# Start-up casting loads that wait for the first plain load, and row terms read from one copy in DRAM

## The reference

```python
proj = x @ w_in                                              # (b, l, D_PROJ)
q, k, v, f_logit, z_att, z_ssd, xbc, dt_raw = jnp.split(proj, _split_points(PROJ_SIZES), axis=-1)
log_f = jax.nn.log_sigmoid(f_logit + b_forget)
F = jnp.cumsum(log_f, axis=1)                                # (b, l, 8 heads)
s = einsum(q, k) * scale + (F[t] - F[s])                     # causal, softmax over s, times v
att = att * silu(z_att)
...
dt = softplus(dt_raw + dt_bias)
a_cs = cumsum(dt * A, axis=2)                                # inside chunks of 128 positions, 32 heads
decay = exp(where(causal, a_cs[l] - a_cs[s], -inf))
y = (C.B * decay) @ (x * dt) + state terms + d_skip * x      # then silu(z_ssd) gate and group RMSNorm
...
h = concatenate([att, y]) @ w_out
x = layer_norm(alpha * x + h, ln_g, ln_b)
```

## Time and profile before

| | us |
|---|---|
| median of 3 runs (lowest 1677.67) | 1677.75 |
| own time of the profiled execution | 1675.15 |
| its span on the slowest core, first to last instruction | 1673.6 |
| spans of the eight cores | 1664.3 to 1673.6 |
| PE busy on the slowest core | 1635.6 (98%) |
| DVE, POOL, ACT busy | 1135.5, 883.6, 849.6 |
| share of the DMA engines, q1 and q0 | 31.4% and 23.5% |

### The profile page before, as it was taken

How to read it: one execution, slowest core, us unless ns; L and a number is a source line. 1 busy time by engine, 2 the same in 40 slices (tenths; PEclk the granted TensorE clock), 3 DMA queues, 4 the chain that set the end, 5 groups by cost and what they waited for, 6 DMA issues and landing times.

```text
span 1673.6 us, 31910 instructions; the slowest of 8 cores (1664.3 to 1673.6 us)
## 1 busy us (share of the span) xinstructions
PE 1635.6 (98%) x9108; PEld 801.4 (48%) x9108; DVE 1135.5 (68%) x2342; ACT 849.6 (51%) x1979; POOL 883.6 (53%) x1377
## 2 busy tenths in 40 slices
PE   5999999999999999999999999999999999999997
PEld 2454544544555455445554455455545544444443
DVE  2676777767876887678668876777778666444444
ACT  2767665665665666666666666666566610000000
POOL 2164564655664667468556765656567523222221
PEclk9999999999999999999999999999999999999999
DMA  9955954593457345644652473239556776445431
GB/s 169 149 79 92 134 97 93 114 123 91 104 103 131 81 92 110 112 97 85 126 87 73 89 139 64 54 77 157 110 112 126 197 194 189 138 139 139 139 95 76
DMA packets 180538, 191.33 MB, mean 114 GB/s; under 512 B 118828, under 2 KB 137132, under 8 KB 175980
## 3 DMA queue, kind: packets, MB, share of 16 engines
q1 hardware_dynamic: 164348, 126.89, 31.4%
q0 software_dynamic: 16016, 62.40, 23.5%
HBM read 198.74 MB, written 39.85 MB: 143 GB/s over the span
## 4 chain that ended last, share of the span: by engine, by line
PE 92%; DMA 4%; issue 1%; DVE 1%; ACT 1%; SPq 0%; POOL 0%; another core or an unknown queue 0%; DVEq 0%; ACTq 0%; POOLq 0%
PE bank L544 91%; DMA mixd<-att 1%; DMA xq<-xT 1%; DMA rowb<-arowd 1%; DMA mixd<-yn 1%; DMA xtok<-xsf 0%; SPq L603 0%; DVE xt L577 0%; PE bank L833 0%; ACT L555 0%; SPq L605 0%; PE bank L762 0%; ACT u L555 0%; ACT dec L555 0%; DVE acc L577 0%
## 5 line engine op out<-in xcount | busy, mean ns | idle before, releaser
L544 PE MATMUL bank<-xq,slab 128*128 128x512 bf16 x3072 | 726.0, 380 | 0.0
L544 PE MATMUL bank<-slab,xq 128*128 128x512 bf16 x2048 | 480.7, 379 | 1.1 <-DMA slab<-wpack 1.1
L544 PEld LDWEIGHTS bank<-xq,slab 128*128 128x128 bf16 x3072 | 293.9, 98 | 304.9 <-issue 3.9
L577 DVE SCALAR_TENSOR_TENSOR acc<-u,cst,acc 128x512 f32<-128x512 f32 x384 | 328.1, 857 | 51.5 <-ACT acc L555 38.8
L544 PEld LDWEIGHTS bank<-slab,xq 128*128 128x128 bf16 x2048 | 197.2, 98 | 211.4 <-issue 1.5
L555 ACT ACTIVATE dec<-rowb,nb 128x128 bf16<-128x128 f32 x512 | 202.2, 397 | 28.1 <-PE bank L544 16.2
L555 ACT ACTIVATE P<-bank,boff 128x512 bf16<-128x512 f32 x192 | 131.1, 683 | 68.7 <-PE bank L544 67.8
L544 PE MATMUL bank<-wo,mTa 128*128 128x512 bf16 x704 | 163.7, 379 | 0.0
L555 ACT ACT_TABLE_LOAD x14 | 18.0, 1283 | 273.6 <-DVE st L1169 270.3
L577 DVE SCALAR_TENSOR_TENSOR xt<-xt,bank 128x512 f32<-128x512 f32 x64 | 43.9, 685 | 141.1 <-PE bank L544 140.8
L566 POOL TENSOR_TENSOR xdd<-xtok,dtde 128x256 bf16<-128x256 bf16 x120 | 83.1, 692 | 85.3 <-PE bank L544 62.9
(11 more groups left out here) (113 smaller groups left out, 2197.8 us busy)
## 6 DMA issues: line engine op xcount, KB each, us to landing
slab<-wpack POOLq DMA_DIRECT2D x80, 512.0 KB, 8.7
rowb<-arowd SPq DMA_DIRECT2D x128, 256.0 KB, 4.0
xt<-x_tok SPq DMA_DIRECT2D x16, 1024.0 KB, 5.0
out<-xt SPq DMA_DIRECT2D x15, 1024.0 KB, 4.3
gbc<-growd SPq DMA_DIRECT2D x32, 256.0 KB, 5.2
mixd<-yn SPq DMA_DIRECT2D x128, 64.0 KB, 2.3
xq<-xT POOLq DMA_DIRECT2D x15, 512.0 KB, 33.8
wo<-w_out POOLq DMA_DIRECT2D x11, 512.0 KB, 9.6
```

Of the source, the lines that this page charges most:

```text
L544: fns.append(lambda e, o=o, a=a, b=b, s=s, t=t: e.matmul(o, a, b, start=s, stop=t))
L577: return p.op("dve", [lambda e: e.scalar_tensor_tensor(out=o, in0=a, scalar=s, in1=b, op0=op0, op1=op1)], dve_us(n, nptr) + (0.12 if nptr ...
```

## The change

Every one of the 21 start-up loads gets `behind=sfb`, which becomes `after=`: it must wait for the last writer of `sfb`, the load of `sf`, and for the readers recorded by then, the two casts of `sf` into `fdtw`. Later calls of `slab_load` and `x_load` have no `behind` and stay as they are. `growd` and `arowd` lose the dimension of copies, `copy_rows` and `copies` go, and every read of a row takes the one row for all 128 partitions, behind its store alone.

```diff
-    growd = nc.dram_tensor("growd", [16, 8, L], F32, kind="Internal").ap()
-    arowd = nc.dram_tensor("arowd", [16, 16, 32, 128], F32, kind="Internal").ap()
+    growd = nc.dram_tensor("growd", [8, L], F32, kind="Internal").ap()
+    arowd = nc.dram_tensor("arowd", [16, 32, 128], F32, kind="Internal").ap()
...
-    def slab_load(name, prio, gate=()):
+    def slab_load(name, prio, gate=(), behind=()):
...
-            1 << 20, 300.0 if prio < -990 or name[1] > 1 else 230.0, after=pro_bufs if s >= NSLOT else ())
+            1 << 20, 300.0 if prio < -990 or name[1] > 1 else 230.0, after=pro_bufs if s >= NSLOT else behind)
...
-    def x_load(q, j, prio, gate=()):
+    def x_load(q, j, prio, gate=(), behind=()):
...
-            "xq%d_%d" % (q, j), list(gate), [b_xq[q][j]], prio, 1 << 20, 300.0 if q < 2 else 230.0)
+            "xq%d_%d" % (q, j), list(gate), [b_xq[q][j]], prio, 1 << 20, 300.0 if q < 2 else 230.0,
+            after=behind)
...
-            x_load(it[0], it[1], n - 1000)
+            x_load(it[0], it[1], n - 1000, (), sfb)
         else:
-            slab_load((it, 0), n - 1000)
+            slab_load((it, 0), n - 1000, (), sfb)
...
-    def copy_rows(q, t, gate):
-
-        qs = slice(q * 512, (q + 1) * 512)
-        a = arowd[:, 4 * q:4 * q + 4, :, :].rearrange("k c (g h) l -> (c g) k (h l)", h=4)
-        DMA("sp", [(growd[1:16, :, qs], growd[0:1, :, qs].to_broadcast([15, 8, 512])),
-                   (a[:, 1:16, :], a[:, 0:1, :].to_broadcast([32, 15, 512]))],
-            "rows%d" % q, [b_row1[q], gate], [b_row[q]], t, 1228800, 100.0)
...
-        DMA("sp", [(gb[:, :], growd[ks, i, g * 512:(g + 1) * 512].unsqueeze(1).to_broadcast(shape))], "gbc%d" % r, [brow],
+        DMA("sp", [(gb[:, :], growd[i:i + 1, g * 512:(g + 1) * 512].to_broadcast([128, 512]))], "gbc%d" % r, [b_row1[g]],
...
-            DMA("sp", [(rb[:, :], arowd[ks, c, h4, :].rearrange("k h l -> k (h l)").unsqueeze(1).to_broadcast(
-                shape))], "rowb%d" % k3, [brow], [brb], t - 14, 262144, 200.0)
+            DMA("sp", [(rb[:, :], arowd[c:c + 1, h4, :].rearrange("k h l -> k (h l)").to_broadcast(
+                [128, 512]))], "rowb%d" % k3, [b_row1[q]], [brb], t - 14, 262144, 200.0)
...
-        if i == 1:
-            copy_rows(q, T[0] + 40, b_mix_att[1][q])
```

More of the change, by code:

```diff
@@ L677, in build_program @@
     b_mix_y = [[Buf("my%d_%d" % (g, c)) for c in range(16)] for g in range(8)]
-    b_row = [Buf("rows%d" % q) for q in range(4)]
     b_row1 = [Buf("row%d" % q) for q in range(4)]
-    def copy_rows(q, t, gate):
-        qs = slice(q * 512, (q + 1) * 512)
-        a = arowd[:, 4 * q:4 * q + 4, :, :].rearrange("k c (g h) l -> (c g) k (h l)", h=4)
-        DMA("sp", [(growd[1:16, :, qs], growd[0:1, :, qs].to_broadcast([15, 8, 512])),
-                   (a[:, 1:16, :], a[:, 0:1, :].to_broadcast([32, 15, 512]))],
-            "rows%d" % q, [b_row1[q], gate], [b_row[q]], t, 1228800, 100.0)
-    def copies(i, q):
-        return (slice(0, 1), [1, 128, 512], b_row1[q]) if i < 2 else (slice(0, 16), [16, 8, 512], b_row[q])
     def xpiece(q, j):
@@ L743, in prologue_quarter @@
         qs = slice(q * 512, (q + 1) * 512)
-        DMA("sp", [(growd[0, :, qs], cs[0:8, :]),
-                   (arowd[0, 4 * q:4 * q + 4, :, :].rearrange("c p l -> p c l"),
+        DMA("sp", [(growd[:, qs], cs[0:8, :]),
+                   (arowd[4 * q:4 * q + 4, :, :].rearrange("c p l -> p c l"),
                     cs[32:64, :].rearrange("p (c l) -> p c l", c=4))], "row%d" % q, [bc], [b_row1[q]], pr, 81920, 30.0)
@@ L895, in attention @@
         gb, bgb = GBC[r]
-        ks, shape, brow = copies(i, g)
-        DMA("sp", [(gb[:, :], growd[ks, i, g * 512:(g + 1) * 512].unsqueeze(1).to_broadcast(shape))], "gbc%d" % r, [brow],
+        DMA("sp", [(gb[:, :], growd[i:i + 1, g * 512:(g + 1) * 512].to_broadcast([128, 512]))], "gbc%d" % r, [b_row1[g]],
             [bgb], base - 20, 262144, 200.0)
@@ L971, in ssd @@
         nw, bnw = NW[0]
-        ks, shape, brow = copies(i, q)
         car, bcar = CAR[0]
```

## The result

The changed kernel takes 1703.8 us (median of 4 runs, 1702.37 to 1705.63) beside 1678.7 us of the kernel before in the same job: a ratio of 1.0153, 95% interval 1.0137 to 1.0169, or 25.7 us more (0.0153 x 1678.7). That is inside 2%, but the time lies above the predicted range (1671.7 to 1682.0).

What follows compares the result with a forecast made beforehand. TensorE bounds the kernel, busy 1635.63 of core 1's 1673.60 us, behind the start-up load queue. Hold -0.5, copies -0.1, row reads 0 and order 0 sum to -0.6 us: 1677.1 us from 1677.75, range 1671.7 to 1682.0.

Steps and rivals of the forecast that it cites:

- The hold: Start: GpSimd's first casting load waits until about 8.0, q0's first packet comes at 10.0; the queue ends 0.5 us earlier.
- lower bound of 9.3: Start: earliest first q0 packet after the held issue, 1.3 us later as for a lone load, leaving no gap.
- rival 2: Start: first casting packet takes 5.25 us again, the queue comes 2.8 us later, 1680.4 us; chance 0.16.
- the 1.1 us: Start: gain of the casting queue because its 255 packets from 6 to 16 are cheaper when unmixed with plain ones.
- the forecast's 0.5 us earlier: Start-up queue: gain of 1.1 us from unmixed packets less a gap of 0.6 us before the first casting packet.
- rival 3: Start: order only, packets no cheaper unmixed, so the gap makes it 0.6 us later, 1678.2 us in all; chance 0.12.
- The copies: Four times two transfers within DRAM go; slowest core gains 0.1 us, its distance to core 5, bound 1.5.
- the stall of SP: SyncE stands 16.0 us, up to 376.38, until the store of `att` lands; removing this gains the slowest core 0.1 us.
- The reads of one row: Head groups 2 to 7: 120 loads cost 0.4 us more each, covered by buffers filled ahead; cost 0, uncovered 48 us.
- Rival 4: Head groups 2 to 7: one DRAM row is too slow under load, losing 4.9 us, 1682.0 us in all; chance 0.10.
- The order: All engines to the end: new start times move neighbours; value 0, bounds -4.9 and +4.9 from small stalls of 100 to 430.
- 910 of 910: From 430 to 1340: TensorE busy 910 of 910 us before, and expected to stay so as a sign of being right.

Runs made afterwards that it cites:

- the run without the gate: Kernel before in its exact order, no hold; only the four copies' wait for the store of the attention output is dropped: ratio 0.9996.
- 16 parts: Kernel before in its exact order with its copying; groups 2 to 7 read copy 0 only, in the shape 16 by 8 by 512: ratio 1.0101.
- the other order: Kernel before with no change of work; the scheduler's assumed rate for start-up input loads is 290 for 300, giving a new order: ratio 1.0108.
- Three new orders: Kernel before, order made anew with the hold alone (1.0086), an assumed load rate of 290 for 300 (1.0108), or a VectorE margin of 0.06 for 0.05 (1.0063).

## Why the prediction was wrong

**The hold: right in what it does, its gain not there.** GpSimd's first load was issued at 7.4 to 8.6, 8.0 on average over the cores (predicted 8.0). The first packet of q0 came at 10.2 on average (predicted 10.0), but that mean is met by luck: on four cores it came at 8.9 to 9.1, under the lower bound of 9.3, and on the other four at 11.2 to 11.5, past the 10.5 from which rival 2 decides. From 9 to 16 on core 2, one of the early ones:

```profile
q0 software_dynamic: 273, 1.03, 92.6%
```

That is 0.926 x 112 / 273 = 0.380 us a packet, where the sum put 0.347: unmixing saves about half of the 1.1 us. The third load lands at 23.6 on average (before 21.3; predicted 21.8). The last of the 21 lands at 96.3 with the hold in the order of before (91.4 to 100.0 on the cores) and at 96.7 without it (93.2 to 98.9), so the end does not clearly come earlier. The Trainium skill's page "DMA: Bandwidth & Descriptors" (section "Queues, rings and completion order") has each engine take turns between the queues that have work; by that rule a hold changes the order of the work and not its sum, and these two landings agree. The run itself measures 1.2 us more (-3.5 to +5.7), which cannot tell the forecast's 0.5 us earlier from rival 3's 0.6 or rival 2's 2.8 later. In the changed kernel the last of the 21 lands at 100.5, and PE stands 1.6 us longer before 100 than before; no run tells what of that is the order.

**The copies: right as far as it was tested.** 0.1 us was predicted for the stall of SP, bound 1.5; the run without the gate measures -0.7 us (-4.2 to +3.0). The copies themselves were taken out only together with a new order.

**The reads of one row: the failed step with a right mechanism beside it.** "Buffers filled ahead of use cover it. Cost 0" was wrong; alone they cost some 16 us. The price, 0.4 us a load, came from quiet stretches, and from the earlier trace rows it was known that three such loads took 17.3 us in a crowd. That was read as the crowd's doing alone. Under load the packets go from 114 to 166 ns and more, loads of over 12 us become seven times as many, and stores, slabs and transposes beside them come late too. The cover that the prediction counted on was that of the rows; what PE then waits for is a transpose or a slab. Rival 4 named the slow row under load, and PE idle after 430 came as its sign, though not behind `rowb`; its size, 4.9 us, was the stalls of the first two groups in the *order of before*, and so three times too small. What neither counted is the slowest core: over the runs behind the ratio the mean of the eight spans grows by 7.7 us, and the longest of them by 16.0 (6.7 and 14.5 with 16 parts), as a late transfer hits some cores of an execution and not others: in its profile four of the eight had a stall of over 1.5 us after 430.

**The order: the failed step that was not seen at all.** "Bounds -4.9 and +4.9, value 0" took the small stalls of 100 to 430 as the scale. But a stall that is seen in one order is no bound for another: in the order of before the `yn` store of 14.2 us just met a user 14.2 us away, and row reads of 20.7 to 26.1 us on every core from 160 to 225 never stopped PE there for over 2.4 us at a time. The bound should have come from the lateness itself: where such a store came later than its user in the other orders, VectorE lost 9.9 to 11.8 us on the cores shown and PE 7.3 to 9.3. Three new orders cost 10.6 to 18 us, and on all cores nearly alike: 13.4, 12.4 and 9.8 us in the mean of the eight spans, 15.3, 15.7 and 10.1 in the longest.

**The sum.** Order 0.0086 (the hold's; that of the changed kernel was never timed alone) and rows 0.0094 to 0.0101 add to 0.0180 to 0.0187; the change measures 0.0153. Within their intervals they add. On the average core they add as well: 13.4 and 7.7 are 21.1 us, and the mean span of the changed kernel, 1691.7, is 20 to 25 us above that of the kernel before in the other jobs (1667.2 to 1671.6). What falls short of the sum is the longest span, perhaps because the two causes need not hit the same core; that is argued. The stretch that the prediction held for safe, 430 to 1340 with "910 of 910", lost 16.4 us on core 3.

What stays open: why the `yn` store lands later in the other order, and why row reads as long as those of before stop PE in one order and not in the other. How the loss of the changed kernel splits between rows and order is not known, beyond the argued half after 640. No version ran clearly faster than the kernel before; reading four rows in place of 16 equals it.

## What to carry to other kernels

Where the order of instructions is made from modelled times, any edit that shifts a start time is two changes: its own, and a new order. Time the edit once with the old order kept and time one or two orders without an edit, before the difference is put down to the edit. When a transfer gets slower, price it by the late tail in the most crowded stretch, its own and that of the transfers beside it, against the work that lies ahead of their first users, and not by its mean in a quiet one. Look at the slowest core and at the mean of the cores: here the rows' cost grew most on the slowest core, and that of an order on all alike.

## What was not expected of the hardware

- 128 partitions that read one 2 KB row of DRAM are much slower under load: 166 to 190 ns a packet against 114 with 16 rows; four rows, 154 ns, lost no time. In a quiet stretch the difference was only 3.6 against 3.2 us a load.
- The slower row reads make other transfers late: from 430 to 1310, in the same order, slabs of over 12 us went from 11 to 30 of 400, and a transpose from under 10 to 25 us and more on three cores.
- A plain transfer whose slowest dimension is 4 kept the DMA engines at a share of 0.2 to 0.3, and the kernel at a ratio of 1.0176, although its packets were the fastest of all (99 ns).
- A stall of PE costs more than its length: around one of 9.3 us, from 192.3 to 201.5, the granted clock was 0.50 (1.2 GHz) from 196.8 to 207.0, 0.92 as the mean of 65 us, and the products of the changed kernel's core 3 took 9.0 us longer in sum.
